# Turning the latent attention's keys before its queries: which of two scalings TensorE waits for first

## The reference, cut to what matters

```
q = (rms_norm_2(cq, q_a_norm) @ w_q_up).reshape(b, s, 8, 96)
kv = (rms_norm_2(ckv, kv_a_norm) @ w_kv_up).reshape(b, s, 8, 64 + 64)
k = concatenate([k_nope, broadcast(k_rope)], -1)
q = rope_tail(rms_norm_2(q, q_norm), positions)
k = rope_tail(rms_norm_2(k, k_norm), positions)
mla = causal_softmax_attention(q, k, v, 96 ** -0.5)
sb = stick_breaking_attention(sq, sk, sv)
return concatenate([mla, sb], -1) @ w_o
```

## Time and profile before

| | us |
|---|---|
| median of 3 runs (lowest to highest) | 931.94 (931.56 to 932.06) |
| the profiled execution | 932.34 |
| its span, first to last instruction | 930.5 |
| busy in the span: PE | 910.7 |
| busy in the span: DVE | 601.1 |
| busy in the span: ACT | 497.8 |
| busy in the span: POOL | 42.7 |

### The profile page before, as it was taken

How to read it: one execution, slowest core, us unless ns; L and a number is a source line. 1 busy time by engine, 2 the same in 40 slices (tenths; PEclk the granted TensorE clock), 3 DMA queues, 4 the chain that set the end, 5 groups by cost and what they waited for, 6 DMA issues and landing times.

```text
span 930.5 us, 14263 instructions
## 1 busy us (share of the span) xinstructions
PE 910.7 (98%) x5396; PEld 771.8 (83%) x5396; DVE 601.1 (65%) x1026; ACT 497.8 (54%) x867; POOL 42.7 (5%) x77
## 2 busy tenths in 40 slices
PE   8999999999999999799999999999999999999998
PEld 5999888899899898667888888887776788888886
DVE  5887778674756778678555554556888665555443
ACT  5468534555565657466444444545676664444441
POOL 2003300000000013000000000010000000000000
PEclk9999999999999999999999999999999999999999
DMA  9545421646334455124556655554442455555560
GB/s 332 186 137 167 122 87 61 212 147 235 128 127 164 158 172 180 46 92 137 183 186 188 192 187 189 184 184 160 158 136 91 133 184 181 180 181 182 185 197 23
DMA packets 106295, 148.25 MB, mean 159 GB/s; under 512 B 12564, under 2 KB 59344, under 8 KB 106112
## 3 DMA queue, kind: packets, MB, share of 16 engines
q1 hardware_dynamic: 104334, 145.61, 48.5%
q0 software_dynamic: 704, 1.77, 0.5%
q10 hardware_dynamic: 1202, 0.13, 0.1%
HBM read 146.03 MB, written 1.45 MB: 158 GB/s over the span
## 4 chain that ended last, share of the span: by engine, by line
PE 87%; DVE 8%; ACT 3%; issue 1%; DMA 1%; SPq 0%; DVEq 0%; ACTq 0%
PE ps L1880 25%; PE ps L1882 25%; PE ps L1881 25%; PE ps L1980 4%; DVE wlo L1175 3%; ACT whi L668 1%; DVE xn L1451 1%; DMA raw<-in_a_w_in 1%; PE ps L2125 1%; PE ps L2281 1%; DVE G L1347 1%; PE ps L2489 1%; PE ps L2520 0%; PE ps L2064 0%; PE ps L2083 0%
## 5 line engine op out<-in xcount | busy, mean ns | idle before, releaser
L1175 DVE TENSOR_TENSOR wlo<-raw,whi 128x1024 fp32r<-128x1024 f32 (+1 forms) x271 | 320.3, 1223 | 211.5 <-ACT whi L668 211.3
L668 ACT ACTIVATE whi<-raw 128x1024 fp32r<-128x1024 f32 (+1 forms) x271 | 270.4, 1047 | 269.0 <-PE ps L1882 268.9
L1880 PE MATMUL ps<-whi,xh 128*128 128x512 f32 (+1 forms) x544 | 217.7, 400 | 1.3 <-DVE wlo L1175 1.0
L1882 PE MATMUL ps<-whi,xl 128*128 128x512 f32 (+1 forms) x544 | 211.8, 389 | 0.0
L1881 PE MATMUL ps<-wlo,xh 128*128 128x512 f32 (+1 forms) x544 | 211.6, 389 | 0.0
L1880 PEld LDWEIGHTS ps<-whi,xh 128*128 128x128 f32 x544 | 102.2, 188 | 23.3 <-issue 3.4
L1882 PEld LDWEIGHTS ps<-whi,xl 128*128 128x128 f32 x544 | 102.1, 188 | 21.6
L1881 PEld LDWEIGHTS ps<-wlo,xh 128*128 128x128 f32 x544 | 102.4, 188 | 18.6
L1880 PE MATMUL ps<-xh,whi 128*128 128x256 f32 x384 | 111.8, 291 | 1.1 <-DVE xl L1241 0.8
L1882 PE MATMUL ps<-xh,wlo 128*128 128x256 f32 x384 | 108.6, 283 | 0.0
L1881 PE MATMUL ps<-xl,whi 128*128 128x256 f32 x384 | 108.5, 283 | 0.0
(11 more groups left out here) (394 smaller groups left out, 1160.0 us busy)
## 6 DMA issues: line engine op xcount, KB each, us to landing
raw<-in_l_w_gate SPq DMA_DIRECT2D x44, 512.0 KB, 3.8
raw<-in_l_w_up SPq DMA_DIRECT2D x44, 512.0 KB, 4.7
raw<-in_l_w_down SPq DMA_DIRECT2D x44, 512.0 KB, 4.5
raw<-in_l_w_in SPq DMA_DIRECT2D x36, 512.0 KB, 4.3
raw<-in_a_w_in SPq DMA_DIRECT2D x32, 512.0 KB, 4.6
raw<-in_w_kv SPq DMA_DIRECT2D x16, 512.0 KB, 4.7
raw<-in_b_w_in SPq DMA_DIRECT2D x16, 512.0 KB, 4.4
raw<-in_l_w_o SPq DMA_DIRECT2D x16, 512.0 KB, 4.4
```

The source lines that it names most:

```text
L668: nc.scalar.activation(whi[:, g % HIGH, a], raw[:, g % RAW, a], ACT.Copy).then_inc(hi_done, 1)
L1175: nc.vector.tensor_tensor(wlo[:, g % LOW, a], raw[:, g % RAW, a], whi[:, g % HIGH, a].bitcast(F32), ALU.subtract).then_inc(lo_done, 1)
L1880: mm(o_, a_h, b_h, start=start, stop=False, skip_group_check=True)
L1882: return mm(o_, a_l, b_h, start=False, stop=stop, skip_group_check=True)
```

## The change

The pairs keep their slots and banks, but their order is turned by four: the n-th pair transposed is pair (n + 4) % 8, so the keys come first. PE waits for the scaled keys before the first pair and for the scaled queries before the fifth. POOL gives a signal of its own when the rotation of the queries is done (`k_rope` to NT + 1), waits for it itself, and the scaling then brings `k_rope` to NT + 2. ACT and DVE wait for that new signal before each eviction, since the turned keys lie over `m_rope`.

```diff
+        turned_pair = lambda n: (n + 4) % 8
...
-            def turned(to, r1, r2, sin, cos, tmp):
+            def turned(to, r1, r2, sin, cos, tmp, done=None):
...
                 nc.gpsimd.tensor_tensor(to[0], tmp[0], tmp[1], ALU.subtract).then_inc(S("pool_chain"), 1)
-                link(nc.gpsimd.tensor_tensor(to[1], tmp[2], tmp[3], ALU.add))
+                if done:
+                    pool.wait_ge(S("pool_chain"), links[0])
+                    nc.gpsimd.tensor_tensor(to[1], tmp[2], tmp[3], ALU.add).then_inc(done, 1)
+                else:
+                    link(nc.gpsimd.tensor_tensor(to[1], tmp[2], tmp[3], ALU.add))
...
-            turned((r1, r2), r1, r2, sin, cos, m_rope)
+            turned((r1, r2), r1, r2, sin, cos, m_rope, S("k_rope"))
+            pool.wait_ge(S("k_rope"), NT + 1)
             pool.wait_ge(*past("mqk", "root", 1))
...
-                for f in at_slot_of(M_TURN, s - 1):
-                    if f % 2 == 0:
-                        act.wait_ge(S("m_T"), f + 1)
+                for n in at_slot_of(M_TURN, s - 1):
+                    if n % 2 == 0:
+                        f = turned_pair(n)
+                        act.wait_ge(S("m_T"), n + 1)
+                        act.wait_ge(S("k_rope"), NT + 1)
                         nc.scalar.activation(m_qkT[0:MLA_QK, 2 * f:2 * f + 2, :].rearrange("p a t -> p (a t)"),
-                                             ps[0:MLA_QK, 4 + f % 2, :], ACT.Copy).then_inc(S("m_Ts_a"), 1)
+                                             ps[0:MLA_QK, 4 + n % 2, :], ACT.Copy).then_inc(S("m_Ts_a"), 1)
...
-                for f in at_slot_of(M_TURN, s - 1):
-                    if f % 2:
-                        dve.wait_ge(S("m_T"), f + 1)
+                for n in at_slot_of(M_TURN, s - 1):
+                    if n % 2:
+                        f = turned_pair(n)
+                        dve.wait_ge(S("m_T"), n + 1)
+                        dve.wait_ge(S("k_rope"), NT + 1)
                         nc.vector.tensor_copy(m_qkT[0:MLA_QK, 2 * f:2 * f + 2, :].rearrange("p a t -> p (a t)"),
-                                              ps[0:MLA_QK, 4 + f % 2, :]).then_inc(S("m_Ts_d"), 1)
+                                              ps[0:MLA_QK, 4 + n % 2, :]).then_inc(S("m_Ts_d"), 1)
...
-                for f in at_slot_of(M_TURN, s):
-                    if f == 0:
+                for n in at_slot_of(M_TURN, s):
+                    f = turned_pair(n)
+                    if n == 0:
                         pe.wait_ge(S("sb_p"), 1)
-                        pe.wait_ge(S("k_rope"), NT + 1)
                         pe.wait_ge(S("m_read"), 2 * NT + 1)
-                    if f >= 2:
-                        pe.wait_ge(S("m_Ts_a" if f % 2 == 0 else "m_Ts_d"), f // 2)
-                    for n in range(4):
-                        last = nc.tensor.transpose(ps[0:MLA_QK, 4 + f % 2, P * n:P * n + P], m_qk[:, n % 2, 2 * f + n // 2, :], ident)
+                    if n == 4:
+                        pe.wait_ge(S("k_rope"), NT + 2)
+                    if n >= 2:
+                        pe.wait_ge(S("m_Ts_a" if n % 2 == 0 else "m_Ts_d"), n // 2)
+                    for i in range(4):
+                        last = nc.tensor.transpose(ps[0:MLA_QK, 4 + n % 2, P * i:P * i + P], m_qk[:, i % 2, 2 * f + i // 2, :], ident)
                     last.then_inc(S("m_T"), 1)
```

## The result

The change made the kernel slower by a little: 933.14 us median of 22 runs (931.42 to 935.20) against 931.53 of 22 runs of the kernel before; the ratio is 1.0017, with an interval of 1.0011 to 1.0023. The prediction was 932.0, 930.7 to 932.7, so it missed. The ratios, with their 95% intervals, need not be the quotient of the two medians to the last digit.

| mean clock | runs of 22 | time, us |
|---|---|---|
| 1.000 | 2 | 931.42, 931.78 |
| 0.998 | 12 | near 933.0 |
| 0.996 | 8 | near 934.7 |

A forecast was written before the change was run, and what follows sets the result against it. PE was taken to bound the kernel, with 87% of the span's chain. The terms −1.25 + 1.25 + 0.04 = +0.04 gave 932.38 for the profiled execution, less 0.40 to the median: 932.0 us, range 930.7 to 932.7.

The forecast's parts named there:

- Parts 1 to 3: First transposes start 1.25 us earlier; PE's stop before the suffix sums grows from 1.32 to 2.56; ACT only idles; net 0.00.
- Part 4: Before the fifth pair: the moved wait for the scaled queries costs 0, as POOL is done 9.0 us before.
- Parts 5 and 6: Added waits of ACT and DVE before evictions cost 0.04, at most 0.70; POOL's extra wait in the rotation costs 0.
- The reading that DVE stood still beside POOL: One DVE operand subtraction took 3.184 us, median 1.220, inferred to be held by POOL's query scaling.
- rival A: DVE's stretched subtraction shortens with PE's stop, so the suffix sums start up to 1.86 earlier: 930.1, or 930.7; chance 0.09.
- Rival B: PE's clock falls to 1.2 GHz behind the 2.56 stop, costing +3.8 (935.8) to +7.6 (939.6); chance 0.03.
- part 2: PE's stop before the suffix sums, released by DVE, grows from 1.32 to 2.56 and gives back 1.25.
- The 0.2% that a measurement was said to tell from no change: For the whole kernel's time, a measurement was taken to tell about 0.2%, 1.86 us, from no change.

The follow-up runs named there:

- experiment 1: The changed kernel with PE again waiting for POOL's scaling before the first pair, order and added waits kept; 931.71 us, ratio 0.9999 to the kernel before.
- experiment 4: The changed kernel with POOL's query scaling held until DVE has masked the third group's logarithms; 929.45 us, ratio 0.9981.
- experiment 3: The changed kernel with 6 useless PE transposes added in the stop before the suffix sums; 932.64 us, ratio 1.0009.
- experiment 5: The changed kernel with POOL's late scaling and 12 useless transposes before the ninth head's turn in the forgetting attention; 929.32 us, ratio 0.9966 to the kernel before.
- experiment 8: The kernel before, queries first, with one more PE wait that puts six matmuls behind a longer stop; 935.16 us, ratio 1.0031.

## Why the prediction was wrong

- **Parts 1 to 3, the stop moves and the gain is given back: right.** Transposes forecast at 372.70, measured 372.23 + 0.50 = 372.73 in the time of the trace before. Second stop forecast 2.56, measured 2.53. L2341 unmoved. DVE's pair 4.32 as before; ACT only idles longer, 4.29.
- **Part 4, the queries' own wait: right.** The fifth pair comes at 384.04, POOL is done at 373.34, and PE does not wait there.
- **Parts 5 and 6, the added waits: right within what can be told.** I took 0.04 with a far end of 0.70; experiment 1 holds all of them and has a ratio of 0.9999, 0.9990 to 1.0008. The 0.04 itself is too small to be seen, and the two executions of the changed kernel at full clock took 931.42 and 931.78, like the kernel before.
- **The reading that DVE stood still beside POOL: right**, and shown by experiment 4. That also answers rival A: the stretch is POOL's, and it goes only when POOL's instruction moves. A's price of 1.86 was measured there as 1.87.
- **Rival B was what happened, and its chance of 0.03 is the step that failed.** The mechanism stood there with its place, and with its sign, a granted clock below 1.00 behind 377.7; but the sum has no term for the clock, and part 2 counts the longer stop as idle time that only moves. In its place the runs showed 1.65 us lost at the lower level behind the stop of 2.53, in about nine of ten executions. The row on idle gaps in the Trainium skill's page "TensorE: Matmul & The Clock Gate", section "Why this matters for your kernels", spoke for B. The runs agree with it in what follows a gap, a clock at half (0.50 behind the stop of 2.53); the stops here are shorter than the gap that the row names, and there the runs decide. I put B aside because the clock was 1.00 at the stop of 1.65. But that was one execution. In a kernel with the same stop there the clock did fall behind it, as the windows of experiment 3 show and the shares of experiments 4 and 5 suggest; and the runs of before that I had, three, all near 931.9, could not show it. One row at 1.00 was taken for a rule, when it was one draw.
- **B's price was too large as well.** I gave +3.8 to +7.6, half or all of 7.59 us of PE work at the lower level. Measured: 1.65 in the profile, about 1.5 between the groups of times, since the full level was back shortly after 381.2. With that price B gives 932.0 + 1.5 = 933.5, outside the range that I had cut off without it. The rest of the way to 933.14 is the base: the 931.94 of three runs became 931.53 with 22.
- **The 0.2% that a measurement was said to tell from no change was too coarse.** 22 runs of each kernel told a change of 0.17% from none, with an interval of 0.11% to 0.23%.

## What to carry to other kernels

Taking a wait away from PE where the next stop takes the gain back need not be free: here two short stops became one long one, and the clock fell behind it. So ask of every gain that is given back how long PE then stands still in one piece and what other stops lie close by, and read the clocks of many executions, not of one profile, before calling a stop harmless. The better edit was to move the instruction that made the next stop: freed from its place by the new order, POOL's scaling could go to where DVE does not feel it, and that let the next stop end 1.87 us earlier in the trace and took the median from 931.55 to 929.45.

## What the runs showed of the hardware

PE's clock fell to its lower level behind single stops as short as 1.64 us in some executions (one was profiled, in experiment 3), behind 1.85 in 4 of 11, and behind 2.50 in 10 of 11. One fall cost 1.65 us in the profile of the changed kernel; in experiment 8 the lower level lasted about twice as long. Two stops of 1.41 and 1.30 with six matmuls between them left the clock at 1.00 in the profiled execution. Useless transposes in a stop kept the clock up: 20 of 22 executions of the changed kernel lost some, 4 of 11 with 12 transposes at the first place, and none of 11 fell to 0.996 with 12 at the second, against 8 of 22.

An elementwise instruction of POOL and one of DVE, both with two operands in SBUF, stood still for each other: the same subtraction took 3.18 beside POOL's scaling and 1.22 without it, and the scaling 4.27 beside DVE's and 2.77 without. The addition of a mask to scores in PSUM (L1699, L1708) was not stretched: it took 0.69 beside POOL's scaling in the kernel before and 0.70 in experiment 4.
